# Modulation of the first block: where x is loaded and scaled, and which engine multiplies the eighth tile of w_ada

## What is computed

```python
cond = jax.nn.silu(c)                                  # c: (1, 1024)
mod = cond @ w_ada[layer] + b_ada[layer]               # (1, 6 * 1024)
sh_m, sc_m, g_m, sh_f, sc_f, g_f = [m[:, None, :] for m in jnp.split(mod, 6, axis=-1)]
h = rms_norm(x, norm_mix[layer]) * (1.0 + sc_m) + sh_m
x = x + g_m * hybrid_mixer(h, w_in[layer], ...)
```

## Time and profile before

| | us |
|---|---|
| median of three runs | 3185.11 |
| lowest and highest | 3181.0, 3193.13 |
| the profiled execution | 3190.7 |
| its span, first to last instruction | 3188.9 |
| TensorE busy in the span | 2993.1 (94%) |
| VectorE busy | 2117.9 (66%) |
| ScalarE busy | 1586.0 (50%) |
| GpSimd busy | 271.4 (9%) |
| mean granted clock of TensorE, of 1 | 0.955 |

### The profile page before, as it was taken

The page is one execution under the profiler, slowest core; times in us unless marked ns, Lnnn a source line. Parts: engine busy times, 40 slices in busy tenths (PEclk is TensorE's granted clock), DMA queues, the critical chain, the costliest instruction groups (busy, mean ns, idle before and its releaser), DMA issues. The chain is left out here.

```text
span 3188.9 us, 46401 instructions
## 1 busy us (share of the span) xinstructions
PE 2993.1 (94%) x18622; PEld 2405.6 (75%) x18622; DVE 2117.9 (66%) x2176; ACT 1586.0 (50%) x1764; POOL 271.4 (9%) x221
## 2 busy tenths in 40 slices
PE   5999999789999999999999967888999999989999
PEld 4777787468878777887787746877778887778877
DVE  6567654569989999989999964566353345356643
ACT  3556433357777777777777642222453442333321
POOL 0110010001111111111111001431000000000000
PEclk9999999789999999999999988989999988999999
DMA  6322343369999999999999941001211112323321
GB/s 248 121 86 83 106 149 119 125 249 374 369 371 377 369 371 368 370 375 374 368 373 365 353 149 53 4 4 39 71 60 58 58 55 76 110 79 93 93 88 70
DMA packets 217372, 607.95 MB, mean 191 GB/s; under 512 B 10784, under 2 KB 118304, under 8 KB 183424
## 3 DMA queue, kind: packets, MB, share of 16 engines
q1 hardware_dynamic: 202480, 554.87, 47.0%
q0 software_dynamic: 14592, 50.36, 4.7%
q10 hardware_dynamic: 144, 0.53, 0.0%
HBM read 582.62 MB, written 23.10 MB: 190 GB/s over the span
## 5 line engine op out<-in xcount | busy, mean ns | idle before, releaser
L2472 DVE TENSOR_TENSOR weight_ring_part<-weight_ring,weight_ring_part 128x2048 fp32r<-128x2048 f32 x380 | 852.8, 2286 | 106.9 <-ACT weight_ring_part L2411 106.5
L2411 ACT ACTIVATE weight_ring_part<-weight_ring 128x2048 fp32r<-128x2048 f32 x380 | 714.4, 1915 | 257.0 <-PE ps L193 136.2
L193 PE MATMUL ps<-weight_ring_part 128*128 128x512 f32 x1456 | 585.3, 402 | 0.0
L293 DVE TENSOR_TENSOR weight_ring_part<-weight_ring,weight_ring_part 128x2048 fp32r<-128x2048 f32 x111 | 253.2, 2281 | 243.2 <-ACT weight_ring_part L290 240.4
L189 PE MATMUL ps<-weight_ring_part,gathered_hi 128*128 128x512 f32 x1024 | 409.0, 399 | 0.0
L193 PE MATMUL ps<-weight_ring_part,gathered_hi 128*128 128x512 f32 x1024 | 405.5, 396 | 0.0
L192 PE MATMUL ps<-weight_ring_part,gathered_lo 128*128 128x512 f32 x1024 | 405.3, 396 | 0.0
L189 PE MATMUL ps<-h1T_hi,weight_ring_part 128*128 128x512 f32 x872 | 363.2, 417 | 3.2 <-DVE weight_ring_part L293 1.7
L192 PE MATMUL ps<-h1T_hi,weight_ring_part 128*128 128x512 f32 x872 | 352.1, 404 | 0.0
L193 PEld LDWEIGHTS ps<-weight_ring_part 128*128 128x128 f32 x1456 | 280.2, 192 | 70.3
L290 ACT ACTIVATE weight_ring_part<-weight_ring 128x2048 fp32r<-128x2048 f32 x111 | 211.1, 1902 | 144.9 <-PE ps L193 106.8
(11 more groups left out here) (489 smaller groups left out, 4466.2 us busy)
## 6 DMA issues: line engine op xcount, KB each, us to landing
weight_ring<-in_w SPq DMA_DIRECT2D x190, 2048.0 KB, 8.9
weight_ring<-in_w_in SPq DMA_DIRECT2D x58, 1024.0 KB, 5.3
weight_ring<-in_w_ffn_up SPq DMA_DIRECT2D x44, 512.0 KB, 4.5
weight_ring<-in_w_ffn_down SPq DMA_DIRECT2D x11, 1024.0 KB, 4.7
mod_tile<-in_w_ada POOLq DMA_DIRECT2D x36, 256.0 KB, 3.1
weight_ring<-in_w_ada SPq DMA_DIRECT2D x8, 1024.0 KB, 12.9
gate_rows<-in_w_ada POOLq DMA_DIRECT2D x28, 256.0 KB, 3.1
weight_ring<-in_w_branch SPq DMA_DIRECT2D x6, 1024.0 KB, 5.2
```

The source lines that it names most:

```text
L193: return nc.tensor.matmul(out, x[0], y[1], start=False, stop=stop)
L293: self.nc.vector.tensor_tensor(lo, full, hi, ALU.subtract).then_inc(self.split, 1)
L2411: nc.scalar.activation(hi_half(h), full_half(h), ACT.Copy).then_inc(w_rounded, 1)
L2472: nc.vector.tensor_tensor(lo_half(h), full_half(h), hi_half(h), ALU.subtract).then_inc(w_split, 1)
```

## The change

Three edits in the first stage. The four loads of x stand behind the load of tile 4 and ahead of those of tiles 5 to 7. VectorE sums over tiles 0 to 6 alone, and raises `mod_summed` once, with the sum over tile 6; TensorE multiplies tile 7 itself, sixteen matmuls with the tile as the stationary operand and `cond[:, 7]` as the moving one, into `ps[:, 1, :]`, behind the sixteen of `mod_sum`; VectorE adds the two results. The reciprocals are taken behind the small work of tile 5, and the pieces of x are scaled two behind tile 5's sum and two behind tile 6's.

```diff
                     if c == 1:
                         sp.dma_start(cols[:, :], a["columns"]).then_inc(small_loaded, 16)
-                for t in range(TT):
-                    sp.dma_start(x_tok[:, t, :], a["x"][0, P * t:P * t + P, :]).then_inc(x_loaded[t], 16)
+                    if c == 4:
+                        for t in range(TT):
+                            sp.dma_start(x_tok[:, t, :], a["x"][0, P * t:P * t + P, :]).then_inc(x_loaded[t], 16)
...
                 for b in range(16):
-                    pe.wait_ge(mod_summed, b // 8 + 1)
+                    pe.wait_ge(mod_summed, 1)
                     last = nc.tensor.matmul(ps[:, 0, b:b + 1], mod_sum[:, P * b:P * b + P], ones[:, 0:1], start=True, stop=True)
+                last.then_inc(picked, 1)
+                pe.wait_ge(cond_ready, 1)
+                pe.wait_ge(tile_loaded[DK - 1], 16)
+                for b in range(16):
+                    last = nc.tensor.matmul(ps[:, 1, b:b + 1], ring.buf[:, 3 + DK, P * b:P * b + P], cond[:, DK - 1:DK], start=True, stop=True)
                 last.then_inc(picked, 1)
...
-                for c in range(1, DK):
+                for c in range(1, DK - 1):
                     dve.wait_ge(tile_loaded[c], 16)
                     dve.drain()
-                    if c < DK - 1:
-                        nc.vector.scalar_tensor_tensor(mod_sum, ring.buf[:, 4 + c, :], cond[:, c:c + 1], mod_sum, ALU.mult, ALU.add)
-                    else:
-                        for h in range(2):
-                            part = slice(1024 * h, 1024 * h + 1024)
-                            nc.vector.scalar_tensor_tensor(mod_sum[:, part], ring.buf[:, 4 + c, part], cond[:, c:c + 1], mod_sum[:, part],
-                                                           ALU.mult, ALU.add).then_inc(mod_summed, 1)
+                    last = nc.vector.scalar_tensor_tensor(mod_sum, ring.buf[:, 4 + c, :], cond[:, c:c + 1], mod_sum, ALU.mult, ALU.add)
+                    if c == DK - 2:
+                        last.then_inc(mod_summed, 1)
...
                         nc.vector.tensor_scalar(a_scale, small[:, 24:28], -8.0, None, ALU.mult)
+                        dve.wait_ge(rooted, 1)
+                        nc.vector.reciprocal(small[:, 8:12], small[:, 4:8])
+                        dve.drain()
+                    if c in (5, 6):
+                        for t in range(2 * c - 10, 2 * c - 8):
+                            nc.vector.tensor_scalar(xn_tok[:, t, :], x_tok[:, t, :], small[:, 8 + t:9 + t], None, ALU.mult)
                 dve.wait_ge(picked, 1)
                 nc.vector.tensor_tensor(mod_cols[:, 0:16], ps[:, 0, 0:16], col("b_ada", 0, 16), ALU.add)
                 dve.drain()
+                dve.wait_ge(picked, 2)
+                nc.vector.tensor_tensor(mod_cols[:, 0:16], mod_cols[:, 0:16], ps[:, 1, 0:16], ALU.add)
+                dve.drain()
                 nc.vector.scalar_tensor_tensor(mod_cols[:, 8:16], mod_cols[:, 8:16], 1.0, col("norm_mix", 0, 8), ALU.add, ALU.mult)
-                dve.wait_ge(rooted, 1)
-                nc.vector.reciprocal(small[:, 8:12], small[:, 4:8])
-                dve.drain()
-                for t in range(TT):
-                    nc.vector.tensor_scalar(xn_tok[:, t, :], x_tok[:, t, :], small[:, 8 + t:9 + t], None, ALU.mult)
```

## The result

The changed kernel took 3196.9 us (median of 20 runs, 3188.69 to 3205.09) against 3187.32 of the kernel before (20 runs): a ratio of 1.0026, 95% interval 1.0018 to 1.0034, which is +8.3 us (5.7 to 10.8); the two medians themselves are 9.6 apart. The forecast was +8.7, a median of 3193.8 within 3185 to 3202. It started from the median of three runs, 3185.1, and twenty runs give 2.2 more for the same kernel. The profiled execution has a span of 3195.1 us.

The account below looks back on a forecast made before the run. TensorE was taken to bound the 3150 us behind the first stage, whose end moves +4.6 (later start), +7.0 (second block), -2.9 (shorter tail), 8.7 us later: 3185.1 + 8.7 = 3193.8 us, range 3185 to 3202.

Parts of the forecast that it names:

- What bounds, and that the shift shows in full: Later stages wait behind the first stage's closing barrier, so its 8.7 us delay would show in full in the whole time.
- Landings: In the first stage's DMA queue, x takes 5.2 us ahead of tiles 5 to 7; tile 5 lands at 25.7.
- VectorE's order: Small operations 1.02, reciprocal 0.3 and two scalings 1.37 us precede the sum over tile 6; TensorE's start moves by 4.6.
- The second block: TensorE's sixteen matmuls on tile 7, behind the first sixteen, cost 6.96 us, +7.0 in the sum.
- both bounds: Second block's cost limits: nothing at all gives +1.7 us; 0.43 us per pass, as dense passes, gives +15.5.
- The start, the tail: First stage: TensorE starts at 33.2 instead of 28.60, +4.6 us; VectorE's tail is 0.45 instead of 3.36, -2.9.
- The queue: Two rivals on SP's queue: x doesn't delay tile 5, +5.6 us, chance 0.08; x's rows block it, +13, chance 0.05.
- The rival of TensorE's clock: TensorE's 64 passes run at the higher clock: +5.3 us throughout, +7.0 if only the second block; chance 0.10.
- Faster: First stage gains some 3 us only with higher clock, earlier start and a nearly free second block; chance 0.01.

Follow-up runs that it names:

- x_early_only: Kernel before with only the loads of x moved behind tile 4; next stage's first DMA 3.9 us later, whole runs 1.0001 (0.9986 to 1.0017).
- tensor_only: Changed kernel with loads of x and scalings put back; next stage's first DMA +5.3 us against the kernel before, whole runs 1.0006 (0.9989 to 1.0023).
- tile7_first: Changed kernel with TensorE's two blocks swapped, tile 7 first; next stage's first DMA 2.0 us earlier than in the changed kernel, whole runs 1.0022.
- no_block2: Changed kernel without TensorE's matmuls on tile 7 and their addition; next stage's first DMA at 41.04 us, 1.3 later than the kernel before.
- dense_after: Changed kernel plus fourteen unused dense matmuls on TensorE ahead of its column sums; next stage's first DMA at 43.60 us, whole runs 1.0022 (1.0010 to 1.0035).
- scale_first: Kernel before with reciprocals and four scalings moved ahead of VectorE's wait for the column sums; next stage's first DMA 2.2 us earlier, whole runs 0.9995.
- dense_ahead: Kernel before plus nine unused dense matmuls on TensorE ahead of the column sums; next stage's first DMA 2.6 us earlier, whole runs 0.9991 (0.9979 to 1.0004).
- combined_busy: Kernel before plus unused dense matmuls ahead of and behind the column sums, scalings ahead of their wait, two on ScalarE; next stage's first DMA 38.38 us, ratio 0.9998.

## Why the prediction was right

*What bounds, and that the shift shows in full.* Right: +8.18 at the barrier and +8.3 in the whole, as far as an interval of 5 us can tell. The next stage added a little: its store of the bias rows is issued 26.6 us behind the barrier and not 25.9.

```profile
65.65 0.32 SPq L626 DMA_DIRECT2D bias_rows<-weight_ring  x1
```

```profile
74.50 0.33 SPq L632 DMA_DIRECT2D bias_rows<-weight_ring  x1
```

The first row is the kernel before, the second the changed one. Among the kernels here that distance lies between 25.2 and 26.6, and it isn't explained; that TensorE's dense passes there become fast at another moment in each would fit, and isn't shown to be the cause.

*Landings.* Tile 5 was to be summed from 25.7 and was from 25.52. x costs its own transfer time ahead of it. Shown by x_early_only.

*VectorE's order.* The small work, the reciprocals and two scalings took 27.79 to 30.38, 2.6, where 2.7 was summed. `rooted` came at 25.8, early, as forecast (26.0).

*The second block.* 6.8 us from the end of the first to its own end, 7.0 forecast; L468's row was the right one to take, and both bounds were far off. Shown by tensor_only, by tile7_first, by no_block2 and by the row itself. The Trainium skill's load time ("TensorE: Matmul & The Clock Gate", LDWEIGHTS) gave an estimated 3.4, which no run here shows at the lower level; at the higher one 32 passes took 3.63.

*The start, the tail.* TensorE starts at 32.88 instead of 33.2, its two blocks take 13.78 instead of 13.92, and VectorE ends 0.47 behind them instead of 0.45. These small excesses make up most of the 0.5 by which the forecast was too long.

*The queue.* Neither rival came true: tile 5 was summed at 25.5, not at 21.5, as it would be if x in front of it cost nothing, and not at 29, as it would be if the small rows of x held up SP's queue.

*The rival of TensorE's clock.* It didn't come true: 64 passes took 13.8 us at one pace. The Trainium skill ("TensorE: Matmul & The Clock Gate", What's actually happening) has the engine leave the lower level under sustained activity; in this case's trace 13.8 us of back-to-back thin passes didn't bring it about, and dense_after shows the level falling during them. But its size was wrong: the transposes' ratio of 0.148 to 0.196 was no measure for thin passes, which go from 218 to 113 ns.

*Faster.* The argument that even a free block would not win holds: no_block2, +1.3.

## What to carry to other kernels

Before an engine is given work, look at when its input is complete and at what stands ahead of it in order: TensorE's idle 28 us lay ahead of the sum, and the added block was put behind it, on the path. And a scaling that waits in program order behind another wait should first be moved past that wait; in scale_first this alone gave 2.2 us at the barrier, without a transfer moved, which is too little to be seen in whole runs (0.9995, 0.9982 to 1.0008).

## What the runs showed of the hardware

In these traces the granted clock doesn't tell the level ahead of its first change. In the kernel before it stands at 1.00 from 45 to 48 us, while dense passes start 0.43 us apart; in dense_ahead, where it had fallen behind the column sums, it stands at 0.50 in the stretch in which they are as slow. So there the level has to be told from the passes' pace. First the kernel before, then dense_ahead (length, TensorE busy, granted clock, DMA share, GB/s), and two of dense_ahead's passes:

```profile
45.00:48.00 3.00, 3.00 (x10) 1.00 1.09 363
```

```profile
41.00:45.00 4.00, 3.57 (x11) 0.50 0.99 327
```

```profile
43.20 0.63 PE L193 MATMUL ps<-weight_ring_part 128*128 128x512 f32 x1
43.63 0.63 PE L189 MATMUL ps<-hT_hi,weight_ring_part 128*128 128x512 f32 x1
```

A pass with one column follows TensorE's clock as a dense one does, 218 ns at 1.2 GHz and 113 at 2.4, but the level didn't outlast such passes: in dense_after it fell in their second block, with the engine 100% busy by its row, and in combined_busy in the last few of the 32 (0.98 in the mean of 28.50 to 32.30, and 0.56 behind it, before the dense matmuls had brought it back).
